# A hybrid encoder layer on one core: moves in the opening, the attention and the recurrent part's end, and the recurrent gates on quarters of the array

## The reference, cut to what matters

```python
xn = rmsnorm(x, g_mix)
u_lru, y_lru, q, k, v, gates = split(xn @ w_in)
xc, _ = causal_dwconv(u_lru, ...)                  # width 4
r = sigmoid(block_diag(xc, w_a, b_a))              # 16 blocks of 64 x 64
i = sigmoid(block_diag(xc, w_i, b_i))
a = exp(-8 * r * softplus(-lam))
h = scan(a, sqrt(1 - a * a) * i * xc)              # along the frames
br_lru = (h * gelu(y_lru)) @ w_br_lru
q, k = rmsnorm per head; attention over 3 chunks of 64 frames with sinks (16 heads, 4 key heads)
x = x + (g0 * br_lru + g1 * (att @ w_br_attn)) @ w_out
...                                                # then a gated MLP of width 3072 with a convolution
```

## Time and profile before

| what | value |
| --- | --- |
| median of three runs | 1793.29 us |
| the profiled execution | 1792.71 us |
| its span (first to last instruction) | 1790.9 us |
| busy: PE, DVE, ACT, POOL | 99%, 47%, 31%, 28% |
| granted TensorE clock | full in all 40 slices |
| beginning to the first values | 0 to 91 us |
| attention blocks | some 121 to 339 us |
| recurrent loop | some 490 to 677 us |
| its end | some 677 to 706 us |

### The profile page before, as it was taken

The page is one execution under the profiler, slowest core; times in us unless marked ns, Lnnn a source line. Parts: engine busy times, 40 slices in busy tenths (PEclk is TensorE's granted clock), DMA queues, the critical chain, the costliest instruction groups (busy, mean ns, idle before and its releaser), DMA issues.

```text
span 1790.9 us, 29796 instructions
## 1 busy us (share of the span) xinstructions
PE 1777.0 (99%) x11192; PEld 1721.9 (96%) x11192; DVE 841.1 (47%) x1626; ACT 561.3 (31%) x1120; POOL 494.5 (28%) x280
## 2 busy tenths in 40 slices
PE   8999999999999999999999999999999999999999
PEld 7998888899999999999999999999999999999999
DVE  7967667511266765113464555312555511555511
ACT  5546544300176674112132333101233200333300
POOL 2121111222333232332233222333332233333222
PEclk9999999999999999999999999999999999999999
DMA  4021010111111111111411111111111111111113
GB/s 163 27 50 32 25 35 25 36 51 47 43 46 38 53 41 36 47 47 47 144 40 43 47 47 47 37 45 48 47 47 47 47 41 41 47 47 47 47 47 122
DMA packets 33090, 90.15 MB, mean 50 GB/s; under 512 B 7536, under 2 KB 12944, under 8 KB 33040
## 3 DMA queue, kind: packets, MB, share of 16 engines
q1 hardware_dynamic: 25664, 82.34, 14.1%
q10 hardware_dynamic: 7376, 7.09, 1.4%
HBM read 83.70 MB, written 4.73 MB: 49 GB/s over the span
## 4 chain that ended last, share of the span: by engine, by line
PE 95%; DVE 3%; ACT 1%; DMA 0%; issue 0%; ACTq 0%; SPq 0%; DVEq 0%
PE banks L449 86%; PE banks L601 2%; PE banks L564 1%; PE banks L531 1%; PE banks L587 1%; PE banks L780 1%; PE banks L781 1%; PE banks L541 1%; DVE x_lo L1280 1%; DVE sqsum L1288 0%; DMA resid<-xT 0%; DVE merged L1288 0%; DVE x_lo L1265 0%; ACT sqsum L1002 0%; DVE resid L1273 0%; ACT pr L978 0%
## 5 line engine op out<-in xcount | busy, mean ns | idle before, releaser
L449 PE MATMUL banks<-x_hi,w_hi 128*128 128x352 f32 x1752 | 578.3, 330 | 4.7 <-DVE x_lo L1265 3.0
L449 PE MATMUL banks<-x_hi,w_lo 128*128 128x352 f32 x1752 | 567.0, 324 | 0.0
L449 PE MATMUL banks<-x_lo,w_hi 128*128 128x352 f32 x1752 | 565.1, 323 | 0.0
L419 POOL TENSOR_SCALAR w_hi<-w_raw 128x1024 fp32r<-128x1024 f32 x136 | 153.6, 1130 | 1216.9 <-DMA w_raw<-W 1216.9
L449 PE MATMUL banks<-h_hi,w_lo 128*128 128x352 f32 x1152 | 372.7, 323 | 0.0
L449 PE MATMUL banks<-h_hi,w_hi 128*128 128x352 f32 x1152 | 372.4, 323 | 0.0
L449 PE MATMUL banks<-h_lo,w_hi 128*128 128x352 f32 x1152 | 371.6, 323 | 0.0
L449 PEld LDWEIGHTS banks<-x_hi,w_hi 128*128 128x128 f32 x1752 | 330.0, 188 | 10.4 <-issue 3.5
L421 POOL TENSOR_TENSOR w_lo<-w_raw,w_hi 128x1024 fp32r<-128x1024 f32 x136 | 332.1, 2442 | 11.4
L449 PEld LDWEIGHTS banks<-x_lo,w_hi 128*128 128x128 f32 x1752 | 329.5, 188 | 3.0
L449 PEld LDWEIGHTS banks<-x_hi,w_lo 128*128 128x128 f32 x1752 | 329.0, 188 | 0.0
(11 more groups left out here) (211 smaller groups left out, 1838.6 us busy)
## 6 DMA issues: line engine op xcount, KB each, us to landing
w_raw<-W SPq DMA_DIRECT2D x137, 512.0 KB, 3.4
sqsum<-xT ACTq DMA_DIRECT2D x2, 2112.0 KB, 13.8
o_yT<-resid SPq DMA_DIRECT2D x7, 528.0 KB, 5.1
resid<-xT SPq DMA_DIRECT2D x4, 704.0 KB, 9.8
resid<-xT SPq DMA_DIRECT2D x4, 352.0 KB, 5.6
w_raw<-W SPq DMA_DIRECT2D x4, 256.0 KB, 5.2
wabs<-wab ACTq DMA_DIRECT2D x8, 128.0 KB, 2.1
o_yT<-resid SPq DMA_DIRECT2D x3, 176.0 KB, 1.8
```

The source lines that it names most:

```text
L419: nc.gpsimd.tensor_scalar(w_hi[s][:, :], w_raw[s][:, :], 1.0, 0.0, ALU.mult, ALU.add).then_inc(w_hi_done, 1)
L449: last = nc.tensor.matmul(out[:, 0:cn], w[s if wt is None else wt][:, k * P:(k + 1) * P], x[:, k, cc:cc + cn], start=(k == 0 and j == 0), ...
```

## The change

In the opening, VectorE makes the third chunk's low part before it ends the first sum of squares; the sums and the spread of the first factors move to other chunks of TensorE's order; GpSimd splits pair 1 first, and the early tile when the third factors are there. `irms` gets a second buffer, and `key_root(1, 1)` moves up on ScalarE. The first attention block's fill grows from 12 to 14 k-steps, later ones shrink. `shift_v` moves from ScalarE's queue to SyncE's, between weight loads. At the recurrent part's end the gates and the chunks are reordered. In `lru_gates` two full products become four of 64 x 64, one for each block, on four different quarters of the array: the input gate's two halves change places, its tanh becomes two instructions that put them back, and its bias is stored exchanged.

```diff
@@ -153,7 +153,7 @@
         h_lo = sb("h_lo", FULL, F32R, at_e)
-        irms = merged[:, 2, :]
+        irms = [merged[:, 2, :], merged[:, 3, :]]
@@ -332,7 +332,7 @@
         SUMS_BLOCKS, SUMS_FROM = (NB - 5, NB - 4, NB - 3), 2
         Q1_BLOCKS, GATE_BLOCKS = 12, 21
-        Q1_STEPS = [12] + 7 * [8] + 4 * [7]
+        Q1_STEPS = [14] + 5 * [8] + 6 * [7]
         Q1_TILES, G_TILES = 4, 6
@@ -388,11 +388,29 @@
             sp.dma_start(w_raw[1][:, :], W[3]).then_inc(wy_loaded, 16)
             sp.dma_start(w_raw[1][:, :], W[5]).then_inc(wy_loaded, 16)
-            with sp.Fori(2, NPAIR - 1) as i:
-
-                for s, (done, loaded) in enumerate(((x_done, wx_loaded), (y_done, wy_loaded))):
-                    sp.wait_ge(done, i * 3 + 3)
-                    sp.dma_start(w_raw[s][:, :], W[bass.ds(i * 2 + (2 + s), 1)].rearrange("a p n -> (a p) n")).then_inc(loaded, 16)
+
+            def shift_v(a):
+
+                n = NC // 2
+                for e, (low, up) in enumerate(((slice(0, n), slice(0, n - 1)), (slice(1, n), slice(0, n)))):
+                    ch = slice(a * P + 64 * e, a * P + 64 * e + 64)
+                    sp.dma_start(vsh[0:CHUNK, low, e, :], vtok[CHUNK:P, 0:low.stop - low.start, ch]).then_inc(s_vsh, 16)
+                    sp.dma_start(vsh[CHUNK:P, up, e, :], vtok[0:CHUNK, 1 - e:up.stop + 1 - e, ch]).then_inc(s_vsh, 16)
+
+            def load_weights(first, last):
+
+                with sp.Fori(first, last) as i:
+                    for s, (done, loaded) in enumerate(((x_done, wx_loaded), (y_done, wy_loaded))):
+                        sp.wait_ge(done, i * 3 + 3)
+                        sp.dma_start(w_raw[s][:, :], W[bass.ds(i * 2 + (2 + s), 1)].rearrange("a p n -> (a p) n")).then_inc(loaded, 16)
+
+            load_weights(2, PAIR_V + 1)
+            sp.wait_ge(v_free, 9)
+            shift_v(0)
+            load_weights(PAIR_V + 1, PAIR_G)
+            sp.wait_ge(a_O, NC)
+            shift_v(1)
+            load_weights(PAIR_G, NPAIR - 1)
             sp.wait_ge(r_lo, START + 3 * KT)
             sp.dma_start(o_h, st_h[:, :, :]).then_inc(s_out, 16)
@@ -422,12 +440,12 @@
             pool.sem_inc(w_hi_done, 2)
+            split(1)
             pool.wait_ge(s_early, 16)
-            pool.wait_ge(x_rlo, 3 * KT)
+            pool.wait_ge(n_dg, 3)
             nc.gpsimd.tensor_scalar(w_hi[2][:, :], early[:, :], 1.0, 0.0, ALU.mult, ALU.add).then_inc(s_ehi, 1)
             nc.gpsimd.tensor_tensor(w_lo[2][:, :], early[:, :], w_hi[2][:, :].bitcast(F32), ALU.subtract).then_inc(e_ready, 1)
-            split(1)
             pool.sem_inc(wx_ready, 1)
             pool.wait_ge(s_w5, 1)
@@ -657,9 +675,8 @@
             unscaled(0, 1)
             pe.wait_ge(s_mat, 16)
-            norm_sums(0)
-            unscaled(1, 1, lambda k: k == 6 and norm_spread(0))
-            unscaled(1, 2)
+            unscaled(1, 1, lambda k: k == 3 and norm_sums(0))
+            unscaled(1, 2, lambda k: k == 3 and norm_spread(0))
                 def before(n, k):
@@ -746,11 +763,11 @@
-                if (n, k) == (0, 2):
+                if (n, k) == (0, 5):
                     pe.wait_ge(s_wab, 16 * KT)
                     lru_gates(KT - 1, 0)
-                elif (n, k) in ((0, 6), (1, 2)):
-                    lru_gates(KT - 1, n + 1)
+                elif (n, k) in ((1, 1), (1, 5)):
+                    lru_gates(KT - 1, 1 + k // 5)
@@ -761,10 +778,11 @@
                 pe.wait_ge(x_act, xa + 3)
                 pe.wait_ge(wx_ready, p0 + 2)
-                for n in range(3):
+                for n in range(2):
                     chunk(0, n, c_hi, d_lo, ks=range(KT - 1))
-                for n in range(3):
+                for n in range(2):
                     chunk(0, n, c_hi, d_lo, last_row(r_lo, START + 3 * (KT - 1), n), ks=range(KT - 1, KT))
+                chunk(0, 2, c_hi, d_lo, last_row(r_lo, START + 3 * (KT - 1), 2))
                 tile(1, 0, p0 + 1, x_hi, x_lo, y_act, ya + 3)
                     tile(0, i, p0 + 2, c_hi, d_lo, x_dve, i * 3 + (xd + 3))
@@ -777,8 +795,12 @@
                 cn = LRU_CHUNKS[n][1]
                 pe.wait_ge(r_tanh, j * 3 + (START + n))
-                nc.tensor.matmul(bank[6][:, 0:cn], wabs[:, 0, :], XC[n][:, 0:cn], start=True, stop=True)
-                nc.tensor.matmul(bank[7][:, 0:cn], wabs[:, 1, :], XC[n][:, 0:cn], start=True, stop=True).then_inc(r_ps, 1)
+                pe.sem_inc(s_own[1], 1)
+                for m in range(2):
+                    for e in range(2):
+                        of, to = slice(HD * e, HD * e + HD), slice(HD * (e ^ m), HD * (e ^ m) + HD)
+                        last = nc.tensor.matmul(bank[6 + m][to, 0:cn], wabs[of, m, of], XC[n][of, 0:cn], start=True, stop=True)
+                last.then_inc(r_ps, 1)
             tile(1, 0, PAIR_R, x_hi, x_lo, y_dve, Y_DVE["G0"])
@@ -955,9 +977,7 @@
                 c0, cn = CHUNKS[c]
                 act.wait_ge(h_ps, m + 1)
-                if m > 2:
-                    act.wait_ge(h_rdy, m - 2)
-                A(irms[:, c0:c0 + cn], bank[6 + m % 2][:, 0:cn], ACT.Sqrt, bias=epsc[:, 0:1], scale=1.0 / HD).then_inc(h_rt, 1)
+                A(irms[a][:, c0:c0 + cn], bank[6 + m % 2][:, 0:cn], ACT.Sqrt, bias=epsc[:, 0:1], scale=1.0 / HD).then_inc(h_rt, 1)
                 act.wait_ge(*((v_done, tt + 1) if tt < 6 else (y_done, 3 * PAIR_V + tt - 5)))
@@ -1012,11 +1032,11 @@
             key_root(0, 1)
             key_root(1, 0)
+            key_root(1, 1)
             head_squares(1, 0)
             act.dma_start(vcs[:, :], vc).then_inc(s_cache, 16)
-            key_root(1, 1)
             last_queries(1)
             for tt in range(6):
@@ -1028,17 +1048,6 @@
             for tt in range(7, 9):
-            def shift_v(a):
-
-                n = NC // 2
-                for e, (low, up) in enumerate(((slice(0, n), slice(0, n - 1)), (slice(1, n), slice(0, n)))):
-                    ch = slice(a * P + 64 * e, a * P + 64 * e + 64)
-                    act.dma_start(vsh[0:CHUNK, low, e, :], vtok[CHUNK:P, 0:low.stop - low.start, ch]).then_inc(s_vsh, 16)
-                    act.dma_start(vsh[CHUNK:P, up, e, :], vtok[0:CHUNK, 1 - e:up.stop + 1 - e, ch]).then_inc(s_vsh, 16)
-
-            act.wait_ge(v_free, 9)
-            shift_v(0)
-
                     if p < PAIR_G:
@@ -1057,8 +1066,6 @@
                     query_root(1)
                     att_hi(g - 1)
-                if g == NB:
-                    shift_v(1)
                 if g + 1 < BLOCKS:
                 if g == 2:
@@ -1127,7 +1134,10 @@
                 ck = slice(c0, c0 + cn)
                 A(FA[:, ck], bank[6][:, 0:cn], ACT.Tanh, bias=halfb[:, cols(j + 2 * KT, 1)], scale=0.5)
-                A(FI[:, ck], bank[7][:, 0:cn], ACT.Tanh, bias=halfb[:, cols(j + 3 * KT, 1)], scale=0.5).then_inc(r_tanh, 1)
+                for e in range(2):
+                    here, there = slice(HD * e, HD * e + HD), slice(HD - HD * e, P - HD * e)
+                    last = A(FI[here, ck], bank[7][there, 0:cn], ACT.Tanh, bias=halfb[there, cols(j + 3 * KT, 1)], scale=0.5)
+                last.then_inc(r_tanh, 1)
                 wait(r_tanh, j * 3 + (START + n + 1))
                 A(row(resid, j, c0, cn), FA[:, ck], ACT.Tanh, bias=lamc[:, 0, cols(j, 1)], scale=lamc[:, 0, cols(j, 1)])
@@ -1322,8 +1332,8 @@
             first_weights_lo(1, 1, wy_ready)
             unscaled_lo(1)
+            unscaled_lo(2)
             x_sums(0, 1)
-            unscaled_lo(2)
             dve.wait_ge(s_mat, 16)
             x_sums(1, 0)
@@ -1349,8 +1359,8 @@
                 c0, cn = CHUNKS[c]
                 dve.wait_ge(h_rt, 3 * a + c + 1)
-                link(D.reciprocal(irms[:, ck], irms[:, ck]))
-                link(D.scalar_tensor_tensor(kG[a][:, ck], kG[a][:, ck], V("g_k"), irms[:, ck], ALU.mult, ALU.mult))
+                link(D.reciprocal(irms[a][:, ck], irms[a][:, ck]))
+                link(D.scalar_tensor_tensor(kG[a][:, ck], kG[a][:, ck], V("g_k"), irms[a][:, ck], ALU.mult, ALU.mult))
                 if c == 2:
                     link(D.tensor_copy(kout[:, a, WIN:WIN + DSEQ], kG[a][:, SMP:T]))
@@ -1725,7 +1735,7 @@
     bg = x["b_gate"][0]
                  conv_w=x["w_lru_conv"][0].reshape(4, KT, P).transpose(2, 1, 0).reshape(P, -1), conv_b=_cols(x["b_lru_conv"][0]),
-                 b_a=_cols(x["b_lru_a"][0]), b_i=_cols(x["b_lru_i"][0]), lam=_cols(x["lru_lambda"][0]),
+                 b_a=_cols(x["b_lru_a"][0]), b_i=np.roll(_cols(x["b_lru_i"][0]), HD, axis=0), lam=_cols(x["lru_lambda"][0]),
                  g_mix=_cols(x["g_mix"][0]), g_ffn=_cols(x["g_ffn"][0]),
```

## The result

The changed kernel takes 1803.36 us (median of 7; 1802.76 to 1805.13), the kernel before, run beside it, 1793.26: a ratio of 1.0055, 95% interval 1.0046 to 1.0064. That is 10 us slower, clear of the interval and just over the 9 us that the prediction set as the least to count. Forecast were 1792.9 us and a range of 1786 to 1798.

The account below looks back on a forecast made before the run. TensorE, busy 99% of 1790.9 us, was taken as the bound, held to ScalarE and VectorE's chain in the changed loop. Beginning -1.6, keys and attention -3.1, loop and end +4.3 gave -0.4: 1792.9 us, range 1786 to 1798.

Parts of the forecast that it names:

- The opening: Start to attention's first products: -2.9 us forecast; 1.6 for the beginning (bounds 0.5 and 2.9), value halves' wait 1.3.
- The attention: Two score waits behind ScalarE's copies, together 1.8 us, go; with the value halves' wait 3.1 us, bounds 1.5 and 3.9.
- free, and up to a block's 6 us if that cover fails: Attention: moving copies to SyncE holds back a gate tile's load, wanted 18 us later against 7 for load and split.
- lower bound (a split on another block): Keys and attention: gain of only 1.5 us, if a GpSimd split now falls on another block.
- Quarters on TensorE: Recurrent gates: four quarter products overlap, 0.92 us a chunk instead of 1.18; 24 x 0.26 = 6.2 us.
- (a): Recurrent gates: quarters run two and two, a chunk costs 1.5 us, total 1797.4 us; chance 0.12.
- (b): Recurrent gates: quarters run one by one, 2.7 us a chunk, 36 us more on TensorE, total 1825; chance 0.05.
- The half tanh: Recurrent loop, ScalarE: each extra tanh charged a full issue step of 0.44 us (0.2 to 0.45), turn 27.2 us.
- Rival (c): Recurrent loop: half tanhs cost the chain nothing, turn 26.0 us at most, total 1782.6; chance 0.07.
- rival (d): Recurrent loop: GpSimd's second split gets ahead of the scan, delaying it 0.6 us net, total 1796.5; chance 0.06.
- The end: Recurrent part's end: gate wait goes, 3.6 us wait for last row comes; loop and end together +4.3 us.
- six more: Recurrent loop: first turn +0.4 us, then six longer turns, moving the last tile's first decay from 679.14 to about 682.5.

Follow-up runs that it names:

- half tanhs alone: Kernel before, full-array gates kept, only the input tanh split into two in-place instructions on 64 partitions each: 1803.34 us, ratio 1.0062.
- the early load: Changed kernel, all work kept, y weights of the recurrent loop's seven pairs loaded early into an idle memory row: 1791.10 us, ratio 0.9987.
- the moves alone: Changed kernel with the old full-array gates and the input tanh in one piece, against the kernel before: 1794.52 us, ratio 1.0007.
- the halves in the other order: Changed kernel with the input tanh's two halves issued in the opposite order: 1804.51 us (one run).
- the quarters alone: Kernel before with only the quarter-array gates and their half tanhs, without the moves: 1803.76 us, ratio 1.0058.
- without the second splits: Changed kernel leaving out loads and splits of seven pairs' y weights beside the loop's scans (stale weights used): 1789.77 us, ratio 0.9980.
- the other end: Early-load version with the last tile's gates reordered and all three join chunks run up to the last row first: 1787.94 us, ratio 0.9971.

## Why the prediction was wrong

**The opening: right.** The waits at the third chunk and the first spread are gone, one at the second spread has come (1.5, forecast 1.3), the value halves' wait is gone; -2.7 against -2.9. That the number fits so closely is luck: the eight traces with this opening pass the place at 124.4 to 127.1 us, three with the old one at 127.4 to 127.9, on average 1.9 us later.

**The attention: the step that failed is "free, and up to a block's 6 us if that cover fails".** The cover held: the delayed load was in time for TensorE. But a load that is late moves its split, and the split came down on VectorE's wanted rows. At the second of the two blocks the changed kernel shows (VectorE, GpSimd, TensorE):

```profile
241.68 2.85 DVE L1403 TENSOR_SCALAR pr<-pr,small 128x128 f32<-128x128 f32 x4
...
241.50 2.35 POOL L439 TENSOR_TENSOR w_lo<-w_raw,w_hi 128x1024 fp32r<-128x1024 f32 x1
...
244.58 0.66 PE L600 MATMUL banks<-mat,pr 128*128 128x128 f32 x4 [1.34 <-DVE pr L1403]
```

The prediction named this as its lower bound (a split on another block) and took 3.1 all the same. Of the attention's 1.8 it gave 0.2; the other traces with these moves say the same (362.5 to 363.7 us from the attention's first products to the loop, 363.3 to 363.8 without the moves).

**Quarters on TensorE: right.** All four run at once; rivals (a) and (b) are out. A chunk's gates add 0.95 us to TensorE's stream, forecast 0.92; a loop that TensorE bounds turns in 26.0, forecast 25.9.

**The half tanh: the term that was mis-sized.** "An activation's issue step is 0.45" was read from two whole activations that overlap by 0.1. The halves do not overlap, and the first, with its halves exchanged, takes the overlap from the decay tanh too: 2.13 us a turn where 3 x 0.44 = 1.32 were charged. Rival (c) is out: the run with the half tanhs alone costs as much as the whole change.

**GpSimd's second split: rival (d), given 0.06, came true beside the forecast.** It should not have stood against the forecast but in its sum: a chain that is later by the half tanhs lets the split come earlier in the chain's time. Its price was 0.3 us a turn above the 2.5 that the chain paid already.

With both, the prediction's own sum is 26.57 - 0.70 + 2.13 + 0.3 = 28.3, against 28.2 measured. TensorE is held to the chain, with waits at the second and third gate: that is as forecast. The chain's length was not, by some 1.0 us in each of seven turns: 6.6 of the 10.5 us by which the total was missed; 1.6 are the attention's, 2.0 the end's. The Trainium skill's TensorEngine Tiling (Array Packing), Performance Considerations, by which the emptying of PSUM may become the bound, agrees with the changed kernel, where the loop waits for the tanhs that empty the gates. With the early load the same tanhs stand there and the loop does not wait for them, so they bound it only together with the collision.

**The end: the mechanism right, 2 us too small.** The wait for the last row came in place of the gate's (2.3 with the hidden 0.16, forecast 3.6). The row's first chunk is the first of these three:

```profile
709.22 1.38 DVE L1547 TENSOR_TENSOR d_lo<-FA,c_hi 128x352 fp32r<-128x352 f32 x3
```

It ends at 709.7, 23.4 us after the first decay (22.8 forecast). The half tanhs are mis-sized here too: from the first decay to ScalarE's root it is 13.5 us (686.31 to 699.82), in the kernel before 11.5 (679.14 to 690.62), 2.0 more where 1.3 were charged. The rest is the clock behind the row: from the end of that wait to the next tile it is 6.5 us (709.78 to 716.27), with the moves alone, at the full clock, 4.9 (700.20 to 705.13). What TensorE lost earlier, 2.2 us at the third gate and the clock behind it, only made the wait for the row shorter.

Two slips in the prediction's sums are small: 705.3 + 0.97 + 3.9 is 710.2, not 710.3, and a turn of 27.2 is 0.5 above the 26.7 of before, as its own "six more" counts, not 0.6.

## What to carry to other kernels

When a second chain runs beside the bounding engine without making it wait, find what its length is made of before adding to it: here 2.5 us of each turn were collisions with another engine that cost nothing until 2 us of other work were added. A load or a DMA that is put elsewhere in a queue moves what it releases; ask on which instruction of the critical chain that then falls, not only whether it is in time. And a saving on one engine that brings extra instructions to another pays only once that one has room: the quarters with their half tanhs lost 10 us as they stood and are worth some 3 with the split out of the way.

## What the runs showed of the hardware

- A tanh on 64 partitions takes as long as one on 128 (0.55 and 0.56 us for 352 columns). Two whole ones follow each other by 0.45, and so does a lower half in place behind a whole one. An upper half behind a lower one, and any half that reads one half of the partitions and writes the other, follows by 0.55 to 0.57. The Trainium skill (ScalarE: Activation LUTs, What ACT_TABLE_LOAD costs) gives an overlap of about 0.09 us for activations in a row: the whole ones agree, these halves do not show it.
- While GpSimd splits, VectorE's instructions with two inputs from SBUF are drawn up to their full length behind it (32 columns of scan: 0.25 us alone, 2.35 beside), so are scaled rows with one input (four of them 0.88 alone, 2.85 and 3.43 beside), and GpSimd's behind VectorE's (a copy of 1.05 us takes 2.55). The Trainium skill (SBUF — State Buffer, Who interferes with whom) has an exclusive lock for a whole instruction; the rows agree.
- After waits of TensorE at the recurrent part's end its clock often fell to its lower level: products 0.29 us apart, ten or eleven of them, beginning at the wait's end in one case and 0.5 to 1.4 us behind it in the others. That is so behind eight of eleven listed waits of 1.9 to 3.5 us: two each in the changed kernel, with the early load and with the halves in the other order, one each with the quarters alone and without the second splits. Behind the other three, of 1.9 us without the second splits, 2.0 with the other end and 2.4 with the moves alone, it did not fall in the traced execution, nor in the loop after waits of 1.1 to 1.3. What decides was not settled.
